# A finer table of job sizes for the mixture-of-experts stage: 16 sizes in place of 12

## The reference: what is computed

```
logits = h2 @ w_router + b_router
top_vals, top_idx = top_k(logits, 4);  gates = softmax(top_vals)
hid = h2[tokens of e] @ w1[e] + b1[e]              # 1024 -> 2048
y   = clamped_swiglu(hid) @ w2[e] + b2[e]          # 1024 -> 1024
x[tokens of e] += gate * y
```

## Time and profile before

| | before |
|---|---|
| median of 3 runs | 1998.32 us |
| the profiled execution | 1999.35 us |
| its span, first to last instruction | 1997.6 us |
| mean granted clock of TensorE | 0.987 |
| wide jobs, 501.06 to 1298.60 us | 797.54 us |
| slim and narrow jobs, 1298.60 us to the end | 699.00 us |

### The profile page before, as it was taken

One profiled execution on the slowest core, in us unless ns is written; L12 is line 12 of the kernel. 1 busy time (PEld: TensorE's weight loads), 2 busy tenths in 40 slices (PEclk: granted clock), 3 DMA queues, 4 the chain that ended last, 5 costly groups with the idle time before them and its releaser, 6 DMA issues.

```text
span 1997.6 us, 33413 instructions
## 1 busy us (share of the span) xinstructions
PE 1923.2 (96%) x12288; PEld 1402.9 (70%) x12288; DVE 1342.6 (67%) x3731; ACT 430.5 (22%) x926; POOL 236.0 (12%) x317
## 2 busy tenths in 40 slices
PE   7999999997999999999999999989998999999996
PEld 5667777773999999999999999933434444444442
DVE  2777777774277777778876777754545766777765
ACT  1233332331121222222222222222321110000100
POOL 1212222221000111111111111110000000000000
PEclk9999999999999999999999999999999999999998
DMA  9311101013867777777788888889999999999992
GB/s 309 109 42 42 42 12 41 31 32 119 327 204 243 255 244 268 255 264 259 265 278 287 287 305 290 311 300 381 399 388 379 382 364 358 365 368 368 366 356 74
DMA packets 207570, 497.93 MB, mean 249 GB/s; under 512 B 7716, under 2 KB 14928, under 8 KB 199968
## 3 DMA queue, kind: packets, MB, share of 16 engines
q1 hardware_dynamic: 194016, 449.43, 62.3%
q0 software_dynamic: 11200, 39.39, 7.9%
q10 hardware_dynamic: 2304, 8.39, 1.0%
HBM read 469.98 MB, written 27.21 MB: 249 GB/s over the span
## 4 chain that ended last, share of the span: by engine, by line
issue 38%; PE 13%; POOL 1%; DMA 1%; DVE 1%; POOLq 0%; ACT 0%
PE ps_unit L1864 13%; DMA out_dram<-y_rows,idx_cur 1%; POOL x_got L1361 1%; DVE act_T L1642 0%; DVE sig L1640 0%; DVE glu L1632 0%; ACT sig L1457 0%; POOL carrier L1357 0%; PE ps_list L1836 0%; POOL out_dram L1418 0%; POOL out_dram L1373 0%; POOLq L1081 0%; POOLq L1273 0%; DMA x_got<-h_rows,idx_next 0%; POOLq L1409 0%
## 5 line engine op out<-in xcount | busy, mean ns | idle before, releaser
L1864 PE MATMUL ps_unit<-xT,w_slot 128*128 128x136 f32 (+6 forms) x3840 | 523.3, 299 | 2.5 <-DVE xT L1667 2.3
L1864 PEld LDWEIGHTS ps_unit<-xT,w_slot 128*128 128x128 f32 x3840 | 518.2, 197 | 3.2 <-issue 3.0
L1894 PE MATMUL ps_unit<-w_slot,xT 128*128 128x512 f32 x704 | 306.7, 594 | 0.0
L1262 DVE STREAM_TRANSPOSE xT<-x_got 32x256 f32<-32x256 f32 x668 | 291.0, 436 | 19.5 <-DMA x_got<-h_rows,idx_next 10.8
L1864 PE MATMUL ps_unit<-act_T,w_slot 128*128 128x136 f32 (+6 forms) x1920 | 265.4, 300 | 9.0 <-DVE act_T L1642 9.0
L1864 PEld LDWEIGHTS ps_unit<-act_T,w_slot 128*128 128x128 f32 x1920 | 260.7, 192 | 12.4 <-issue 6.3
L1894 PEld LDWEIGHTS ps_unit<-w_slot,xT 128*128 128x128 f32 x704 | 132.8, 190 | 163.0 <-issue 163.0
L1658 DVE STREAM_TRANSPOSE y_rows<-yT 32x256 f32<-32x256 f32 x396 | 172.5, 436 | 40.0 <-ACT yT L1464 34.8
L914 PE MATMUL ps_c<-hT,w_in_sb 128*128 128x128 f32 x1536 | 181.5, 278 | 5.4 <-DMA w_in_sb<-in_w_in_dram 5.4
L914 PEld LDWEIGHTS ps_c<-hT,w_in_sb 128*128 128x128 f32 x1536 | 176.7, 193 | 10.6 <-DMA w_in_sb<-in_w_in_dram 6.2
L1357 POOL TENSOR_TENSOR carrier<-carrier 128x1 f32<-128x1 f32 x64 | 14.9, 233 | 1336.5 <-issue 574.7
(11 more groups left out here) (292 smaller groups left out, 1853.5 us busy)
## 6 DMA issues: line engine op xcount, KB each, us to landing
w_slot<-in_w_dram SPq DMA_DIRECT2D x192, 2048.0 KB, 11.7
b_row<-in_b_dram SPq DMA_DIRECT2D x11, 1024.0 KB, 12.9
w_in_sb<-in_w_in_dram SPq DMA_DIRECT2D x6, 1024.0 KB, 12.0
b_row<-in_b_dram SPq DMA_DIRECT2D x11, 512.0 KB, 15.2
x_in<-in_x_dram SPq DMA_DIRECT2D x8, 512.0 KB, 3.5
x_res<-in_x_dram SPq DMA_DIRECT2D x8, 512.0 KB, 4.7
out_dram<-x ACTq DMA_DIRECT2D x8, 512.0 KB, 4.9
h_rows<-h ACTq DMA_DIRECT2D x8, 512.0 KB, 2.9
```

What stands on the lines that cost most here:

```text
L1262: last = nc.vector.transpose(out[c * Q:(c + 1) * Q, :, tokens], rows.rearrange("p (k c j) -> p k c j", c=P // Q, j=Q)[:, :, c, :])
L1864: last = pe.matmul(ps_unit[p % RING][:, u, 0:n], w, moving[:, k, 0:n], start=(k == 0), stop=(k == KD - 1))
L1894: last = pe.matmul(ps_hid[c], xT[:, k, 0:P], w_slot[:, c, k, :], start=(k == 0), stop=(k == KD - 1))
```

## The change

SIZES gets steps of 4 from 128 to 160 and keeps steps of 8 above: 132, 136, 140, 144, 148, 152, 156, 160, 168, ... 208, 256 follow 128. So there are 16 sizes, 15 of them with code for wide jobs (before: 12 and 11), 4 packed words instead of 3, and `limits` is the larger of two arithmetic series, made by three instructions with a wait between them instead of by one.

```diff
-SIZES = tuple(range(P, 209, SIZE_STEP)) + (CAP,)
+FINE = 160
+SIZES = tuple(range(P, FINE, SIZE_STEP // 2)) + tuple(range(FINE, 209, SIZE_STEP)) + (CAP,)
...
+        limits_made = sem("limits_made")
...
-            nc.vector.tensor_scalar(limits[:, 0, :], cst[:, C_IOTA:C_IOTA + len(SIZES) - 1], float(SIZE_STEP), float(SIZES[0]),
-                                    ALU.mult, ALU.add)
+            places = cst[:, C_IOTA:C_IOTA + len(SIZES) - 1]
+            nc.vector.tensor_scalar(limits[:, 0, :], places, SIZE_STEP / 2, float(P), ALU.mult, ALU.add).then_inc(limits_made, 1)
+            nc.vector.tensor_scalar(limits[:, 1, :], places, float(SIZE_STEP), float(2 * P - FINE), ALU.mult,
+                                    ALU.add).then_inc(limits_made, 1)
+            dve.wait_ge(limits_made, 2)
+            nc.vector.tensor_tensor(limits[:, 0, :], limits[:, 0, :], limits[:, 1, :], ALU.max)
```

More of the change, by code:

```diff
@@ L1562, in _ @@
             one_row = cst[:, C_ONES:C_ONES + P]
-            assert SIZES[:-1] == tuple(SIZES[0] + SIZE_STEP * i for i in range(last_size))
+            assert SIZES[:-1] == tuple(max(P + SIZE_STEP // 2 * i, 2 * P - FINE + SIZE_STEP * i) for i in range(last_size))
             dve.wait_ge(ranked, 1)
```

## The result

The changed kernel took 2004.67 us (median of 20 runs, 2001.13 to 2007.99); the kernel before took 1999.78 us over 20 runs of its own (1997.70 to 2006.32). The ratio is 1.0020, with a 95% interval of 1.0012 to 1.0027: slower by some 4 us (4.9 between the medians), where 2.5 us less was forecast. One later execution of the changed kernel, 3355.51 us at a mean granted clock of 0.555, is left out of every comparison. The profiled execution took 2005.43 us with a span of 2003.6 us, 6.0 more than the span before.

A forecast was written before the change was run, and what follows sets the result against it. PE was taken to bound jobs 10 and 11, DVE to pace jobs 8 and 9. Terms -2.4 (jobs 10 and 11), -0.4 (job 9), 0 (job 8), +0.3 (start) gave -2.5 us: 1998.32 to 1995.8 us, range 1992.9 to 1999.0.

The forecast's parts named there:

- Widths, and the price of a column: Wide jobs: 152 becomes 148 once, 144 becomes 140 three times; four columns save 3.3 ns a matmul, 120.8 ns at 140.
- Jobs 10 and 11: Wide jobs of 140 columns, bounded by PE: 370 matmuls x 3.3 ns, 1.2 us saved each, 2.4 us for both.
- Jobs 8 and 9 paced by DVE and the scatter: Wide jobs 8 and 9: first-layer savings vanish in second-layer pauses; job 8 gains nothing, job 9 0.4 us.
- The start, +0.3 us: Start of the wide stage: fourth word's matmuls and register load mostly hidden in PE's idle time; +0.3 us, at most 1.7.
- One more size, and more that are skipped, taken at nothing: Crossings between wide jobs: one more used size and more skipped ones cost nothing, at most some tenths of a us each.
- The limits, "hidden": DVE at 32.5 us: three instructions and a wait instead of one, hidden behind a 9.32 us wait; 0.5 us without cover.
- Rival B: Start costs its full 1.7 us, skips over 144 and 132 cost 0.5 us each: 1998.2 us; chance 0.13.
- Rival C: Longer pauses of jobs 8 and 9 bring the 1.2 GHz clock into full stream: price taken 1999.5 us; chance 0.07.
- A: Whole width counts: all four narrower wide jobs gain 1.3 us each, -5.1 us, 1993.2 us; chance 0.13.
- D: Table does not do what it says, or counts differ from the reference's; widths as before, 1998.6 us; chance 0.03.

The follow-up runs named there:

- the narrower jobs alone: Kernel before with 12 sizes 128, 136, 140, 148, 152, 160, 168, 176, 184, 192, 208, 256, second-block threshold 140 instead of 144; ratio 0.9994 (0.9983 to 1.0006).
- the kernels with two empty sizes: Kernel before with size 156 in place of 184, so 160 and 156 are both passed over; ratio 1.0010 (0.9998 to 1.0021).
- with the code moved: Kernel before with 128 PE instructions that never run added to the code of size 256; ratio 0.9989 (0.9977 to 1.0002).

## Why the prediction was wrong

- *Widths, and the price of a column*: right. 121.0 ns at 140 columns against 120.8.
- *Jobs 10 and 11*: right, 2.48 us in the traced execution against 2.4.
- *Jobs 8 and 9 paced by DVE and the scatter*: right in kind. Without the gaps (the narrower jobs alone) job 8 gained nothing and job 9 0.3 us; but jobs 7 and 8 together took 0.9 us more than before there, where the prediction allowed 0.5.
- *The start, +0.3 us*: wrong in size and beyond its upper bound of 1.7: +2.70 us, and +0.99 in job 1 by the lower clock behind the gap. The step that failed was "the new matmuls fit into these 2.04 us, if PE's sequencer gets through them in time; what follows at 497.71 waits for a DMA that no one delays." The 2.04 us were not free: PE's branch over 256 ran until 495.1, so 0.9 us were left ahead of 495.99. In the changed kernel it ran until 497.8 and the first transposes started 0.63 us later, counted from the table, waiting for no DMA. The larger part, 2.07 us, came behind that: the matmuls and the load are instructions, and they moved the end of a block of code into the transposes. The earlier trace rows can't show that. The kernel before had very likely waited for a block too, where its trace names DVE's copies as what ended the 2.26 us ahead of its first wide matmul: a 16 KB packet ran until 499.6, the same wait is put down to "issue" in the kernels with two empty sizes and with the narrower jobs alone (2.39 and 2.36 us), and with the code moved the matmul came 0.9 us sooner from the table.
- *One more size, and more that are skipped, taken at nothing*: the second step that failed, the smaller one in these traces (2.2 us net for 156 and 0.6 for 144, against 3.7 for the start with job 1). I read one crossing of one empty size at 858.06 and carried it to two in a row (160 and 156) and to another place (144). They took 4.63 and 2.05 us of PE. The rule of the Trainium skill (Runtime: NRT & Kernel Launch, Instruction fetch mechanics) that I set beside it was the better guide, and I let one row that did not contain the case outweigh it.
- *The limits, "hidden"*: wrong. No wait at 32 us showed them, but PE's waits in the mixer grew by 1.0 us with them, more than the 0.5 us given for no cover at all. Why stays open.
- *Rival B* (the gain is eaten at seams) named the mechanism, at 0.5 us each for the skips of 144 and 132 and nothing for that of 156, and so ended at 1998.2, too low. (The branch over 132 took 0.34 us and PE did not stop there.) With the measured prices it would have read 2.70 for the start, 0.99 for job 1 behind it, 4.80 - 2.62 for the second empty size and 1.36 - 1.54 for 144 with the gains of jobs 8 and 9 in it, less 2.48 for jobs 10 and 11: +3.2 us. With the 1.0 of the mixer it is +4.2, which agrees with the measured 4 us; the single terms are from one trace each, so the closeness is partly luck.
- *Rival C* (the clock): right in kind, wrong in place. In the changed kernel the pauses of jobs 8 and 9 did not grow as forecast, since the gaps had let DVE catch up; the low clock in full stream came at the wide stage's start and behind the gap of 4.63 us (3.4 us at 0.50). In the narrower jobs alone the pause of job 9 did grow, from 2.72 to 3.52 us, and the low clock came behind that of job 8.
- *A and D* fell.

## What to carry to other kernels

A table of variants that are compiled in full costs the engine's code, not only its branches: count how many unused variants stand in a row between used ones, and what a branch over each waits for. Before crediting an edit of a few instructions ahead of a large loop with its own time, test it against padding that never runs; in the changed kernel 128 such instructions were worth 5 to 6 us, more than the change. An instruction taken as hidden at its own place can cost elsewhere: compare the sums of waits of every stage, also of those that the change doesn't touch. And a gap of PE ahead of a stretch that another engine paces costs less than its length, because that engine catches up in it.

## What the runs showed that I had not expected

- A branch over a second empty size in a row took 4.5 to 4.9 us in each of six kernels, over a third 7.2 us; over a first one 0.34 to 1.0 us, but 2.6 to 3.7 us over 144 in four kernels that pass over it directly behind a job of 148 and 0.35 in three others that differ in where the code lies.
- Which alignment is good was not worked out; only two shifts (8 and 128 instructions) were made on purpose.
- One execution differs from another by several us: the kernel before ran from 1995.6 to 2008.3 in these comparisons. The first median shown, of three runs, was 1998.32, that of 20 was 1999.78. Differences under 2 us are read here from the traces only, and each kernel has one.
